# Memory keys and values computed at the stage entries, the norm root ahead of the splits, high and low matmuls grouped, larger first loads

## The reference

```python
def first_block(x, ...):
    h = x
    for layer in range(2):
        hn = rmsnorm(h, norm_mix[layer])
        mix = chunked_band_attention(...) if layer == 0 else rglru_block(...)   # 16 heads; gated linear recurrence
        h = h + mix
        h = h + sq_relu_mlp(rmsnorm(h, norm_mlp[layer]), mlp_w1[layer], mlp_w2[layer])   # 1024 -> 4096 -> 1024
    return rmsnorm(h, norm_final)

def second_block(x, mem, ...):
    h = rmsnorm_2(x, g_pre[i])
    (gq, gk, gv, ga, gz, dq, dk, dv, iq, ik, iw, dz, xq, xz, gates) = split_cols(h @ w_in[i])
    y_gla = gla_mixer(gq, gk, gv, ga, gz, ...)                       # gated linear attention, 4 heads
    y_dsa = dsa_mixer(dq, dk, dv, iq, ik, iw, dz, rel_bias)          # index scores, top 64 keys, 8 heads
    y_mem = cross_mixer(xq, xz, rmsnorm_2(mem, g_mem[i]), w_mem_kv[i])   # mk, mv = split(mem_n @ w_mem_kv)
    merged = s_gla * (y_gla @ w_gla_out) + s_dsa * (y_dsa @ w_dsa_out) + s_mem * (y_mem @ w_x_out)
    return x + rmsnorm_2(merged @ w_o[i], g_post[i])
```

## Time and profile before

| | us |
|---|---|
| median of 3 runs | 1018.02 (1017.8 to 1019.61) |
| profiled execution, its own time | 1019.6 |
| its span | 1018.3 |
| PE busy | 996.3 (98% of the span) |
| DVE busy | 682.5 (67%) |
| ACT busy | 578.7 (57%) |
| POOL busy | 83.1 (8%) |

### The profile page before, as it was taken

The page is one execution under the profiler, slowest core; times in us unless marked ns, Lnnn a source line. Parts: engine busy times, 40 slices in busy tenths (PEclk is TensorE's granted clock), DMA queues, the critical chain, the costliest instruction groups (busy, mean ns, idle before and its releaser), DMA issues.

```text
span 1018.3 us, 13520 instructions
## 1 busy us (share of the span) xinstructions
PE 996.3 (98%) x5222; PEld 838.2 (82%) x5222; DVE 682.5 (67%) x1156; ACT 578.7 (57%) x1008; POOL 83.1 (8%) x85
## 2 busy tenths in 40 slices
PE   8999999999999989999999999999999999999997
PEld 6877788888888987888888888887888888888886
DVE  6867676656667977766566686756566545577564
ACT  6667755445456786555454584457565554575443
POOL 2312110000003330100000000000120010000000
PEclk9999999999999999999999999999999999999999
DMA  9753445555554344455555563554433444335551
GB/s 341 296 188 130 173 165 206 193 201 183 189 203 157 138 165 166 169 203 200 193 200 176 202 248 130 176 205 165 166 125 123 167 132 158 124 108 185 204 186 41
DMA packets 27583, 180.28 MB, mean 177 GB/s; under 512 B 3056, under 2 KB 4080, under 8 KB 6784
## 3 DMA queue, kind: packets, MB, share of 16 engines
q1 hardware_dynamic: 26768, 176.89, 49.2%
q0 software_dynamic: 288, 2.10, 0.5%
q10 hardware_dynamic: 464, 0.44, 0.2%
HBM read 178.37 MB, written 1.05 MB: 176 GB/s over the span
## 4 chain that ended last, share of the span: by engine, by line
PE 81%; DVE 8%; ACT 7%; issue 3%; DMA 1%; SPq 0%; DVEq 0%; ACTq 0%
PE bank L296 20%; PE bank L281 13%; PE bank L283 13%; PE bank L282 13%; PE bank L297 10%; PE bank L299 3%; DVE lo L1254 2%; ACT L L857 2%; ACT hi L771 2%; PE bank L298 1%; DVE L L1327 1%; DVE L L1391 1%; DMA raw<-in_wv 1%; PE bank L435 1%; PE bank L478 1%
## 5 line engine op out<-in xcount | busy, mean ns | idle before, releaser
L1254 DVE TENSOR_TENSOR lo<-raw,hi 128x1024 fp32r<-128x1024 f32 x318 | 379.6, 1242 | 21.3 <-ACT hi L771 21.2
L771 ACT ACTIVATE hi<-raw 128x1024 fp32r<-128x1024 f32 x318 | 319.7, 1050 | 85.9 <-PE bank L283 84.9
L296 PE MATMUL bank<-X,hi 128*128 128x512 f32 x1001 | 362.4, 401 | 1.4 <-DVE zr L1268 1.2
L297 PE MATMUL bank<-X,lo 128*128 128x256 f32 x1001 | 281.6, 281 | 0.0
L296 PEld LDWEIGHTS bank<-X,hi 128*128 128x128 f32 x1001 | 188.9, 189 | 43.2 <-DVE zr L1268 1.8
L297 PEld LDWEIGHTS bank<-X,lo 128*128 128x128 f32 x1001 | 190.0, 190 | 4.5
L803 ACT ACTIVATE bt<-bank 128x256 f32<-128x256 f32 x143 | 54.3, 381 | 159.7 <-PE bank L299 159.5
L1268 DVE TENSOR_TENSOR zr<-bank,bt 128x256 f32<-128x256 f32 x64 | 27.2, 425 | 112.0 <-ACT bt L803 112.0
L281 PE MATMUL bank<-hi,zh 128*128 128x512 f32 x256 | 99.9, 390 | 0.0
L283 PE MATMUL bank<-hi,zl 128*128 128x512 f32 x256 | 99.7, 390 | 0.0
L282 PE MATMUL bank<-lo,zh 128*128 128x512 f32 x256 | 99.7, 390 | 0.0
(11 more groups left out here) (307 smaller groups left out, 1477.8 us busy)
## 6 DMA issues: line engine op xcount, KB each, us to landing
raw<-in_w SPq DMA_DIRECT2D x64, 1024.0 KB, 4.7
raw<-in_rin SPq DMA_DIRECT2D x8, 1024.0 KB, 4.7
raw<-in_wk SPq DMA_DIRECT2D x4, 1024.0 KB, 9.2
raw<-in_wq SPq DMA_DIRECT2D x4, 1024.0 KB, 7.6
raw<-in_wo SPq DMA_DIRECT2D x4, 1024.0 KB, 4.7
raw<-in_mk SPq DMA_DIRECT2D x4, 1024.0 KB, 4.6
raw<-in_rout SPq DMA_DIRECT2D x4, 1024.0 KB, 4.7
raw<-in_mv SPq DMA_DIRECT2D x4, 1024.0 KB, 4.7
```

Of the source, the lines that this page charges most:

```text
L296: PE.matmul(bank[b][:, :], wh[:, c:c + P], both_, start=k_ == 0, stop=False, skip_group_check=True)
L297: return PE.matmul(bank[b][:, 0:S], wl[:, c:c + P], x[:, k_, 0, :], start=False, stop=False, skip_group_check=True)
L771: ACTE.activation(hi[u_ % HIS][:, c], raw[u_ % RAW][:, c], ACT.Copy).then_inc(hi_cut, 1)
L1254: DVE.tensor_tensor(lo[u_ % RAW][:, c], raw[u_ % RAW][:, c], hi[u_ % HIS][:, c].bitcast(F32), ALU.subtract).then_inc(lo_cut, 1)
```

## The change

1. `half` issues its high matmuls of slices 0 to 6 first, then all eight low ones, then the last high one. They wait for the high split first, and for the low split only then.
2. mk 2 moves from ahead of rout to the entry of the recurrence, mv 0 and mv 1 stand ahead of rout, mv 2 and mv 3 at the entry of the second block. rin 0 takes banks 7 and 6, and the buffers bo and rstd_mem move.
3. `token_rstd` of the recurrence's norm stands ahead of the splits of `at_tile("mk", 1)` on ACT; DVE makes x_lows ahead of the splits.
4. The second w1 tile of each MLP takes banks 6 and 7 in place of 4 and 5.
5. Index heads go in pairs, each pair ahead of a half of dk 0 or dq 0, and iw is transposed into bank 1.
6. The first two steps of the sparse mixer have two halves each, the last two a half of gz; DVE's `soft` stands behind the product with the gate; the last turn stands behind the product.
7. `top8` and `decay_sum` stand beside other tiles.
8. The first loads are fewer and larger: hx in pieces of 2, 2 and 4 slices, wv in half tiles.

```diff
@@ plan
-    out += [("wo", i) for i in range(4)] + [("mk", 0)] + mlp_plan(0) + [("mk", 1)]
-    out += [("rin", i) for i in range(8)] + [("mk", 2)] + [("rout", i) for i in range(4)]
-    out += [("mk", 3)] + mlp_plan(1) + [("mv", 0), ("mv", 1)]
+    out += [("wo", i) for i in range(4)] + [("mk", 0)] + mlp_plan(0) + [("mk", 1), ("mk", 2)]
+    out += [("rin", i) for i in range(8)] + [("mv", 0), ("mv", 1)] + [("rout", i) for i in range(4)]
+    out += [("mk", 3)] + mlp_plan(1) + [("mv", 2), ("mv", 3)]
...
+DSA_STEPS = [[("dq", 3, 0), ("dq", 3, 1)], [("xq", 0, 0), ("xq", 0, 1)]]
+DSA_STEPS += [[("xq", i, j)] for i in range(1, 4) for j in range(2)] + [[("gz", 0, 0)], [("gz", 0, 1)]]
+INDEX_STEPS = [("dk", 0), ("dk", 1), ("dq", 0), ("dq", 1)]
@@ half, PE
+            def high(k_):
+                p.wait_ge(hi_cut, cut_at(t, k_ // 4))
...
+            for k_ in ks[:-1]:
+                high(k_)
             for k_ in ks:
-                m = feature(t, x, j, b, k_)
+                p.wait_ge(lo_cut, cut_at(t, k_ // 4))
+                c = k_ * 256 + j * 128
+                PE.matmul(bank[b][:, 0:S], wl[:, c:c + P], x[:, k_, 0, :], start=False, stop=False, skip_group_check=True)
+            m = high(ks[-1])
@@ mlp, PE
-                    cols(f"w1_{n}", i, X2, (4, 5))
+                    cols(f"w1_{n}", i, X2, (6, 7) if i == 1 else (4, 5))
@@ recurrence entry, ACT
         squares("mix1", h, (h_added, 4), 0)
+        token_rstd(NST["mix1"] + 4, 2, NST["mix1"] + 8, 1.0 / D, 2)
         at_tile("mk", 1)
-        token_rstd(NST["mix1"] + 4, 2, NST["mix1"] + 8, 1.0 / D, 2)
         second("mk", 2)
+        second("mk", 3)
         x_highs("mix1", "norm_mix", 8)
@@ ahead of rout, ACT
-        at_tile("mk", 2)
+        at_tile("mv", 0)
         gated(2)
-        second("mk", 4)
         gated(4)
-        second("mk", 5)
-        at_tile("rout", 0)
+        at_tile("mv", 1)
+        copy_tokens(mv, "mv", 0)
         gated(6)
@@ index heads, PE
-        for i in range(4):
-            index_head(i)
-        cols("dk", 0, X2, (4, 5))
-        for i in range(4, 8):
-            index_head(i)
+        for j, (name, e) in enumerate(INDEX_STEPS):
+            index_head(2 * j)
+            index_head(2 * j + 1)
+            half(name, 0, e, X2, 4 + e)
@@ sparse mixer, DVE
                 x.then_inc(freed[4], 1)
-                soft(n, TT)
...
                 DVE.tensor_tensor(tmp[n % 2][:, :], bank[7][:, 0:S], sz[:, n, :], ALU.mult).then_inc(freed[7], 1)
+            if i < 8:
+                soft(16 + i, TT)
@@ first loads, SP
-            j = slice(*((0, 1), (1, 2), (2, 4), (4, 6), (6, 8))[n])
+            j = slice(*((0, 2), (2, 4), (4, 8))[n])
...
+        def half_tile(g_):
+            u_, c = g_ // 2, slice(g_ % 2 * HALF, (g_ % 2 + 1) * HALF)
+            SP.dma_start(raw[u_][:, c], A["wv"][u_][:, c]).then_inc(first_in[g_], 16)
```

More of the change, by code:

```diff
@@ L99, in build @@
     freed = [sem(f"freed{b}") for b in range(8)]
-    x_in = [sem(f"x_in{i}") for i in range(5)]
+    x_in = [sem(f"x_in{i}") for i in range(3)]
     ones_in, vec_in, ident_in, gmask_in, mem_in, h_in = (
@@ L167, in build @@
     L = [small(f"L{i}", [512]) for i in range(2)]
-    PT = [small(f"PT{i}", [512]) for i in range(2)]
+    PT = [small("PT0", [512])]
+    o_pt1 = top[0]
+    PT += [small("PT1", [512])]
     o_bt = region(BT * 1024)
@@ L526, in pe @@
         half("mk", 1, 0, M2, 7)
-        half("mk", 1, 1, M2, 6, range(0, 4))
+        half("mk", 1, 1, M2, 6)
+        half("mk", 2, 0, M2, 4, range(0, 4))
         turned_x("mix1", hn, hn_made, 0)
-        half("mk", 1, 1, M2, 6, range(4, 8))
+        half("mk", 2, 0, M2, 4, range(4, 8))
+        half("mk", 2, 1, M2, 5)
         def gates(n):
@@ L547, in pe @@
             plain("rin", i, X, (2, 3) if i % 2 else (4, 5))
-        half("mk", 2, 0, M2, 6)
-        half("mk", 2, 1, M2, 7)
+        for i in range(2):
+            tokens("mv", i, M, (7, 6))
         for i in range(4):
@@ L588, in pe @@
         tile_end[t] = full["dv", 1]
-        for i in range(3):
+        for i in range(1, 3):
             cols("dq", i, X2, (4, 5))
-        for i in (2, 3):
-            tokens("mv", i, M, (2, 3))
         for i in range(2):
@@ L613, in pe @@
         for i in range(10):
-            name, a, b = DSA_STEPS[i]
-            half(name, a, b, X2, (6, 3)[b])
+            for name, a, b in DSA_STEPS[i]:
+                half(name, a, b, X2, (6, 3)[b])
             if i < 8:
@@ L627, in pe @@
                 weigh(16 + n, bank[7][:, 0:S], dv, c, c + 128).then_inc(done, 1)
-        for i in range(4):
+            if i == 8:
+                turn(16 + i - 1, CAUSAL)
+        for i in range(1, 4):
             cols("gz", i, X2, (4, 5))
@@ L1052, in index_head @@
             ACTE.activation(rl[i % 2][:, :], bank[6 + i % 2][:, 0:384], ACT.Relu).then_inc(free["is", i][0], 1)
-        for i in range(4):
-            index_head(i)
-        kept("dk", 0)
-        for i in range(4, 8):
-            index_head(i)
+        for j, (name, e) in enumerate(INDEX_STEPS):
+            index_head(2 * j)
+            index_head(2 * j + 1)
+            at_half(name, 0, e)
+            second(name, e, scale=128 ** -0.5 if name == "dq" else 1.0)
         at_tile("dv", 0)
@@ L1107, in act @@
         for i in range(10):
-            name, t, j = DSA_STEPS[i]
-            at_half(name, t, j)
-            second(name, 2 * t + j, scale=128 ** -0.5 if name == "dq" else 1.0 / 16)
+            for name, t, j in DSA_STEPS[i]:
+                at_half(name, t, j)
+                second(name, 2 * t + j, scale={"dq": 128 ** -0.5, "xq": 1.0 / 16, "gz": 1.0}[name])
             if 1 <= i <= 8:
@@ L1506, in dve @@
         mlp(1, 3, "rout")
[L1508 removed]
+        lo_to(2 * (T_OF["mv", 2] + 2))
         own()
@@ L1580, in top8 @@
             step(x)
-        for i in range(4):
-            index_head(i)
-        at_tile("dk", 0)
-        kept(dk, "dk", 0)
-        for i in range(4, 8):
-            index_head(i)
+        for j, (name, e) in enumerate(INDEX_STEPS):
+            index_head(2 * j)
+            index_head(2 * j + 1)
+            at_half(name, 0, e)
+            if name == "dk":
+                joined(dk[:, e, :], "dk", e)
+            else:
+                joined(dq[:, e, :], "dq", e, scale=128 ** -0.5)
         d.wait_ge(score_read, 8)
@@ L1592, in dve @@
         top8(0)
-        for i in range(3):
+        for i in range(1, 3):
             at_tile("dq", i)
             kept(dq, "dq", i, 128 ** -0.5)
-            top8(1 + i)
-        for i in (2, 3):
-            at_tile("mv", i)
-            top8(2 + i)
-        at_tile("gq", 0)
-        kept(gq, "gq", 0)
-        top8(6)
-        at_tile("gq", 1)
-        kept(gq, "gq", 1)
+            top8(i)
+        for i in range(2):
+            at_tile("gq", i)
+            kept(gq, "gq", i)
+            top8(3 + i)
+        for i in range(2):
+            at_tile("gk", i)
+            kept(gk, "gk", i)
+            top8(5 + i)
+        at_tile("gv", 0)
         top8(7)
-        at_tile("gk", 0)
-        kept(gk, "gk", 0)
         own()
@@ L1887, in pool @@
             POOL.tensor_tensor(ig[:, n, :], tt[:, n, :], ig[:, n, :], ALU.mult).then_inc(drive_made, 1)
-        for j in range(4, 8):
+        for j in range(6, 8):
             by_rows(mk, "mk", j, "mem", 2, mk_scaled)
```

124 lines of the change are left out of this document (60 added, 64 removed).

## The result

The changed kernel took 1000.61 us (median of 4 runs, 999.91 to 1001.11), the kernel before 1018.82 (4 runs beside it, 1017.80 to 1020.30): a ratio of 0.982 [0.9803, 0.9837]. The forecast was 999.5. The profiled execution took 1000.7, its span 999.4, against 1019.6 and 1018.3: 18.9 us less, where 18.5 were forecast. The sum was nearly right, four of its terms were off by 0.8 to 1.9 us.

A forecast was written before the change was run, and what follows sets the result against it. PE, busy for 98% of the span, was taken to bound the kernel. Terms of 4.6, 0.5, 1.3, 1.1, 0.8, 4.7 and 5.5 sum to 18.5 us, so 1018.0 - 18.5 = 999.5 us; range 993 to 1008.

The forecast's parts named there:

- Term 1: Halves of tiles: grouping high and low matmuls saves 0.035 us in each of 131 halves, 4.6 us, between 0 and 6.6.
- One of the prediction's signs: MLP 0: a pair of a w1 and a w2 tile would take 10.45 us in place of 10.52.
- Rival C: Low matmuls in a row: weight loads not hidden, 0.190 us each, 70 us more, 1074 in all; chance 0.02.
- Term 2: First loads: weights of slices 2 and 3 issued about 1 us sooner, 0.5 us gained; best 1.6, worst 0.8 lost.
- Term 3: w1's second tile in each MLP: free banks remove two waits of 0.6 us and some restart, 1.3 us.
- Term 4: Entry of the recurrence: mk 2 there gains 1.53 less 0.45 for a late low split, 1.1 us, between 0 and 1.8.
- Term 5: Ahead of rout: mv 0 and 1 cover 3.2 us of gl waits, less 2.4 of new waits, 0.8 us.
- Term 6: Index heads: pairs ahead of halves and iw's other bank remove waits and the clock's fall, 4.7 us; at worst 2.
- Term 7: Sparse mixer: DVE's new order and two halves at the ends let PE lead, 5.5 us, between 2 and 6.3.
- Rival B: Recurrence and rout, heads, sparse mixer: removed waits return behind other instructions, half of 11.0 us stays, 1005; chance 0.12.
- Rival D: Whole kernel: clock falls elsewhere, loads start later or rout waits longer; only Term 1 or Term 7 left, about 1013; chance 0.02.

The follow-up runs named there:

- alternate: The changed kernel with high and low matmuls of a half alternating again; 1003.33 us, ratio 0.9845.
- group_only: The kernel before with only the grouped order of matmuls in a half added; 1016.53 us, ratio 0.9973.
- after: The changed kernel itself, with all parts of the change, against the kernel before; 1000.61 us, ratio 0.982.
- old_loads: The changed kernel with the first loads in their old pieces and order; 1002.33 us, ratio 0.9839.
- old_banks: The changed kernel with the second tile of w1 on banks 4 and 5 again in both MLPs; 1002.51 us, ratio 0.9843.
- root_old: The changed kernel with the recurrence's norm root behind ACT's high pieces of mk 1 again; 1000.34 us, ratio 0.9822.
- rout_fix: The changed kernel with ACT's high splits of rout 1 and 2 ahead of the gh copies; 999.94 us, ratio 0.9809.
- heads_old: The changed kernel with index heads in two groups of four and iw in bank 6 again; 1002.91 us, ratio 0.9846.
- soft_first: The changed kernel with DVE's softmax scaling ahead of the product with the gate again in the sparse mixer; 1004.78 us, ratio 0.9858.
- single_steps: The changed kernel with one half in each sparse mixer step, DVE's new order kept; 1001.68 us, ratio 0.9835.
- fixed: The changed kernel with rout_fix's edit, rin 0's first low half ahead of mk 3's join, and xq 0 on banks 2 and 0; 997.92 us, ratio 0.9798.

## Why the prediction was right, and where it was wrong

**Term 1, mechanism right, too big** (4.6; 2.4 to 3.0 measured, by alternate and group_only). The step that failed is "six of the eight at the pure pitch, the two next to the low ones at the old pitch". Start to start in MLP 0 after: high to high and the last high to the first low 0.227, the first low to the second 0.113, then 0.120 to each low and to the high behind them. From that high on the next two starts are 0.233 and 0.236 apart, and three more 0.228 to 0.233, before they settle. So a half takes 0.02 us more than at the pure pitches, where the forecast left 0.012: 2.793 us in place of 2.820 - 0.035 = 2.785. That is 0.027 saved in an MLP, and under half of it elsewhere. One of the prediction's signs was mis-added: a pair of a w1 and a w2 tile takes 2 x 2.82 + 5.44 = 11.08 us before, not 10.52, and 11.03 after. The formula of the Trainium skill (TensorE: Matmul & The Clock Gate, Back-to-back issue gap), columns over 2.4 GHz and 2.5 ns, has nothing of the neighbour in it. The section gives it for the isolated matmul and has 131 ns for 512 columns in a stream with weight loads. Neither is seen here: high matmuls in a row stand 0.227 us apart, and alternate and after, the same by the formula, are 2.35 us apart. Rival C is refuted: the low matmuls stand 0.120 apart with a weight load each.

**Term 2, too small** (0.5; 1.4). The prediction let the weights be issued 1 us sooner and took off for the larger first piece. The third slice was ready two us sooner, and the first matmul, which waits for the larger piece, started at 7.0 us on average over eleven profiles, and at 6.9 over the three with the old loads. Of the 1.4 the loads bring about 1.2 (0.9 by the profile of old_loads, 1.7 by its medians); the rest lies between two executions.

**Term 3, right, with the restart underrated** (1.3; 1.7 by old_banks).

**Term 4, size right (1.1; 1.4), one effect not foreseen.** The late low piece at rin 0 was there: 0.37 where 0.45 was foreseen. That the root's place gives hn nothing was in the prediction; root_old shows that it costs 0.4, since ACT's splits and bt stand behind it.

**Term 5, too small** (0.8; 2.0). The order of events was right: PE waits for DVE's low pieces at rout 1 and rout 2 and not for gl. The sizes were 0.21 and 0.61, nothing at mv 1, in place of 0.7, 1.3 and 0.4; rout_fix prices the two at 1.3 us, not 2.4, and 3.2 - 1.3 = 1.9. Following two in-order streams put ACT and DVE some 0.4 to 0.7 us later than they were.

**Term 6, too big** (4.7; 3.9). The waits went, the clock stayed up. The pair of heads was mis-sized: 0.8 read from four matmuls of one row, where 3.84 - 2.79 = 1.05 is what a pair costs between two halves, four times. heads_old puts 2.5 us of the 3.9 on the order and the bank at full clock (0.9 of it on the bank), which leaves 1.4 for the 3.4 us at 0.50. That share is only argued: no run turned the clock's fall off by itself. The record of the other executions says more. Beside the experiments the kernel before was timed 27 times: 13 executions had a mean clock of 0.998 or 0.999 and took 1017.5 to 1018.4 us, 14 had 0.994 to 0.997 and took 1019.1 to 1021.2. One fall of 3.41 us takes 0.0017 off the mean, so at least the six at 0.999 had none. For the others the mean does not decide, since the clock is at 0.50 at the very end too (from 1015.38 us on in the profile of the kernel before). The profiled execution (0.997, 1019.6) is of the second sort. The forecast took the 1.7 us of the fall off the median of 1018.0 as well, which by its time is of the first sort. An estimate without them is 1018.0 - 16.8 = 1001.2, nearer to the 1000.61 measured than 999.5 is.

**Term 7, right** (5.5; 5.5). soft_first gives 3.7 and single_steps 1.7, 5.4 together; term 1 has almost no part in it, since alternate loses 0.03 in this stretch and group_only gains 0.12. The wait at bank 6 was 0.65 for a forecast of 0.7.

Measured less forecast, the terms were off by -1.9, +0.9, +0.4, +0.3, +1.2, -0.8 and 0, which cancel to 0.1: the sum was better than its parts, by luck. The 0.9 us between dv and the sparse mixer is term 1 again (0.55 by alternate, 0.84 by group_only). Rival B is out, since waits came back only to 1.9 us, in the named places. Rival D is out.

Open: what decides whether the clock falls at the heads. It fell in both profiles of the old order with the old work around it, and by the mean clocks not in every execution of the kernel before. It did not fall in the profile of heads_old, nor, by their mean clocks of 0.999, in two of its other three executions. Open too is how the gains of terms 4 and 5 divide between the moves of mk and mv and the other edits there: they are read from landmarks, and only the root and the order at rout were undone by themselves.

## What to carry to other kernels

Where one engine is 98% busy, time is to be had from short waits, and each is worth more than its idle time: 0.58 shown cost 0.84, 1.84 in four waits 2.8. A late engine's queue is worth following instruction by instruction: four of the five new waits that it named here came, though most were smaller than it said. Such a wait can then be removed by one or two moved lines, as fixed does. Before a term is taken off a median, look whether the profiled execution had something (here a fall of the clock) that the median one did not. Price a group of small matmuls from start to start with its neighbours, not from its own row.

## What the runs showed of the hardware

- Changing between a 512 wide and a 256 wide matmul costs TensorE time in both directions taken together: eight pairs took 2.82 us alternating and 2.79 grouped in MLP 0, with the same matmuls and weight loads; at the pitches of unbroken rows, 0.2267 and 0.120, they would take 2.77.
- The granted clock fell to 0.50 (1.2 GHz) for 3.41 us in two profiles (616.02 to 619.43 in the kernel before, 614.29 to 617.70 in group_only), behind waits of 0.83 and 0.56 us. In heads_old waits of 0.83 and 0.57 stand at the same instructions and the clock stays at 1.00. In the 3.00 us from the iw transposes on, PE is busy 1.60 us in the kernel before, 1.61 in group_only and 1.61 in heads_old. The Trainium skill (TensorE: Matmul & The Clock Gate, Part 1, the HAM clock gate) ties the fall to idle time; the idle time of the waits alone does not tell these kernels apart. The same page calls what a kernel gets at its start "run-variable"; for a fall in its middle the 27 executions of the kernel before point the same way, since a mean clock of 0.999 in six of them leaves no room for one.
- The first real matmul started between 6.5 and 7.7 us in eleven profiles of kernels with the same first loads, and the difference mostly stays to the end: root_old's profile starts 0.74 us later than after's and ends 0.29 later though it is 0.4 faster between.
